# A third staging buffer for gate and up weights in an expert loop, laid over part of the selection tiles

## What is computed

```
scores = sigmoid(xt @ w_router)                    # 16 experts in 4 groups of 4
g_sel  = argmax over groups of the sum of the two best biased scores
gates  = the two best experts of that group, weights normed to sum 1
h = silu(einsum('nd,edf->enf', xt, w_gate)) * einsum('nd,edf->enf', xt, w_up)
h = h * gates.T[:, :, None]                        # D_EXPERT = 256
y = einsum('enf,efd->nd', h, w_down)
```

## Time and profile before

| | us |
|---|---|
| median of 3 runs | 3438.38 |
| lowest, highest | 3436.19, 3446.0 |
| profiled execution | 3443.66 |
| its span | 3441.9 |

### The profile page before, as it was taken

The page is one execution under the profiler, slowest core; times in us unless marked ns, Lnnn a source line. Parts: engine busy times, 40 slices in busy tenths (PEclk is TensorE's granted clock), DMA queues, the critical chain, the costliest instruction groups (busy, mean ns, idle before and its releaser), DMA issues.

```text
span 3441.9 us, 42094 instructions
## 1 busy us (share of the span) xinstructions
PE 3222.5 (94%) x14924; PEld 2551.4 (74%) x14924; DVE 1936.3 (56%) x2968; ACT 1386.9 (40%) x2048; POOL 394.2 (11%) x241
## 2 busy tenths in 40 slices
PE   8899998998999888999988999999999999899998
PEld 6677776676777766888866788877887767678886
DVE  5775776568658765544465644456353553565353
ACT  4553666455536664222223322233222554532221
POOL 3101122331012223000010000010000000010000
PEclk9999999999999999999999999999999999999999
DMA  3101799421018993222312232324233312023232
GB/s 126 48 10 65 236 322 309 132 71 41 19 55 270 323 310 111 83 97 91 98 51 84 71 100 91 101 66 148 90 97 114 108 49 74 25 75 105 85 99 75
DMA packets 174979, 389.59 MB, mean 113 GB/s; under 512 B 11312, under 2 KB 70064, under 8 KB 174192
## 3 DMA queue, kind: packets, MB, share of 16 engines
q1 hardware_dynamic: 173424, 377.45, 33.5%
q0 software_dynamic: 1408, 10.23, 0.8%
HBM read 381.34 MB, written 6.29 MB: 113 GB/s over the span
## 4 chain that ended last, share of the span: by engine, by line
PE 69%; DVE 13%; DMA 9%; ACT 4%; DVEq 2%; issue 2%; POOL 0%; POOLq 0%; ACTq 0%; SPq 0%
PE ps L562 19%; PE ps L564 19%; PE ps L563 19%; DMA gate_up_stage<-in_w_gu 8%; DVE moe_lo L1987 5%; PE ps L751 2%; ACT moe_hi L1170 2%; PE ps L696 1%; PE ps L856 1%; PE ps L729 1%; ACT w_hi L1170 1%; PE ps L687 1%; PE ps L791 1%; PE ps L735 1%; PE ps L809 1%
## 5 line engine op out<-in xcount | busy, mean ns | idle before, releaser
L1601 DVE TENSOR_TENSOR w_lo<-w_stage,w_hi 128x1024 fp32r<-128x1024 f32 (+3 forms) x310 | 398.6, 1287 | 853.9 <-ACT w_hi L1170 852.4
L562 PE MATMUL ps<-xs_hi,w_hi 128*128 128x512 f32 (+2 forms) x1938 | 771.8, 398 | 42.4 <-DVE w_lo L1601 14.7
L1170 ACT ACTIVATE w_hi<-w_stage 128x1024 fp32r<-128x1024 f32 (+3 forms) x350 | 382.3, 1093 | 1013.0 <-PE ps L564 999.3
L564 PE MATMUL ps<-xs_hi,w_lo 128*128 128x512 f32 (+2 forms) x1938 | 765.5, 395 | 0.0
L563 PE MATMUL ps<-xs_lo,w_hi 128*128 128x512 f32 (+2 forms) x1938 | 765.2, 395 | 0.0
L562 PEld LDWEIGHTS ps<-xs_hi,w_hi 128*128 128x128 f32 (+2 forms) x1938 | 365.8, 189 | 141.8 <-issue 22.8
L564 PEld LDWEIGHTS ps<-xs_hi,w_lo 128*128 128x128 f32 (+2 forms) x1938 | 365.9, 189 | 84.2
L563 PEld LDWEIGHTS ps<-xs_lo,w_hi 128*128 128x128 f32 (+2 forms) x1938 | 366.7, 189 | 81.8
L1987 DVE TENSOR_TENSOR moe_lo<-gate_up_stage,moe_hi 128x1024 fp32r<-128x1024 f32 x224 | 270.1, 1247 | 118.7 <-ACT moe_hi L1170 118.1
L1170 ACT ACTIVATE moe_hi<-gate_up_stage 128x1024 fp32r<-128x1024 f32 x224 | 226.4, 1054 | 149.4 <-DMA gate_up_stage<-in_w_gu 139.8
L564 PE MATMUL ps<-h_hi,w_lo 128*128 128x512 f32 x704 | 278.3, 395 | 0.0
(11 more groups left out here) (381 smaller groups left out, 4872.4 us busy)
## 6 DMA issues: line engine op xcount, KB each, us to landing
gate_up_stage<-in_w_gu SPq DMA_DIRECT2D x112, 1024.0 KB, 5.6
w_stage<-in_f_gu SPq DMA_DIRECT2D x174, 512.0 KB, 3.5
down_stage<-in_w_dn SPq DMA_DIRECT2D x112, 512.0 KB, 5.8
w_stage<-in_f_dn SPq DMA_DIRECT2D x64, 704.0 KB, 4.0
w_stage<-in_w_in SPq DMA_DIRECT2D x30, 512.0 KB, 3.6
w_stage<-in_d_qk SPq DMA_DIRECT2D x24, 512.0 KB, 3.5
w_stage<-in_w_out SPq DMA_DIRECT2D x16, 512.0 KB, 3.6
w_stage<-in_d_v SPq DMA_DIRECT2D x12, 512.0 KB, 3.5
```

The lines of the kernel that those rows point to most:

```text
L562: pe.matmul(o, lh, rh, start=start, stop=False)
L564: return pe.matmul(o, ll, rh, start=False, stop=stop)
L1170: copy = lambda o, i: nc.scalar.activation(o, i, ACT.Copy)
L1601: tt(w_lo[:, s, 0:n], stage[:, s, 0:n], w_hi[:, s, 0:n].bitcast(F32), ALU.subtract).then_inc(w_split, 1)
```

## The change

The list of gate and up buffers gets a third, `gate_up_stage2`, of 8 KB a partition. It is placed at the tiles 3 to 6 of `sel_t`, which is also the last 8 KB of `sel`. The transfers, numbered q = 2 st + i, take the buffers 0, 1, 0, 2, 1, 0, 2, 1, ... Each waits for the splitting of the transfer that had its buffer before; the first use of buffer 2 (q = 3) waits for `gt_full`, the last reading of `sel`. On SP `(2, 0)` is issued ahead of the loop, and in the loop the order becomes `(st + 2, 1)`, `down (st + 1, 0)`, `down (st + 1, 1)`, `(st + 3, 0)`. Tiles 0 to 2 of `sel_t` are made in steps 1 to 3 as before; tiles 3 and 4 are made in step 26 and tiles 5 and 6 in step 27, after `moe_lo` unit 4 in step 26 and right after `ht_lo` in step 27. The orders of TensorE, ScalarE and POOL are the same.

```diff
+        gu_stage.append(over(region_s, "gate_up_stage2", [P, 4, 512], at=(NTILES - 4) * T * 4))
...
+        GU_BUFFER = [0, 1] + [(0, 2, 1)[q % 3] for q in range(2 * STEPS - 2)]
+        GU_TURN = [GU_BUFFER[:q].count(b) for q, b in enumerate(GU_BUFFER)]
+        GU_USES = [GU_BUFFER.count(b) for b in range(3)]
...
-        gu_landed = [sem(f"gate_up_landed{i}") for i in range(2)]
+        gu_landed = [sem(f"gate_up_landed{i}") for i in range(3)]
...
                 def gate_up_weights(st, i):
-                    if st > 0:
-                        sp.wait_ge(gu_lo, l * 4 * STEPS + 4 * (st - 1) + 2 * i + 2)
+                    q = 2 * st + i
+                    b = GU_BUFFER[q]
+                    if GU_TURN[q] > 0:
+                        before = max(p for p in range(q) if GU_BUFFER[p] == b)
+                        sp.wait_ge(gu_lo, l * 4 * STEPS + 2 * before + 2)
+                    elif b == 2:
+                        sp.wait_ge(gt_full, l + 1)
...
+                gate_up_weights(2, 0)
                 for st in range(STEPS):
-                    for i in range(2):
-                        if st + 2 < STEPS:
-                            gate_up_weights(st + 2, i)
+                    if st + 2 < STEPS:
+                        gate_up_weights(st + 2, 1)
                     for i in range(2):
                         if st + 1 < STEPS:
                             down_weights(st + 1, i)
+                    if st + 3 < STEPS:
+                        gate_up_weights(st + 3, 0)
...
-                    if 1 <= st <= NTILES:
-                        if st == 1:
-                            v.wait_ge(row_copied, l + 1)
-                        ts(selt[:, st - 1, :], slot_row[:, :], dc[:, C_COL + st - 1:C_COL + st], None, ALU.is_equal).then_inc(selt_ready, 1)
+                    if st == 1:
+                        v.wait_ge(row_copied, l + 1)
+                    for i in {1: (0,), 2: (1,), 3: (2,), STEPS - 2: (3, 4), STEPS - 1: (5, 6)}.get(st, ()):
+                        ts(selt[:, i, :], slot_row[:, :], dc[:, C_COL + i:C_COL + i + 1], None, ALU.is_equal).then_inc(selt_ready, 1)
```

More of the change, by code:

```diff
@@ L159, in build_program, with staged @@
         gu_stage = [over(at_stage, "gate_up_stage0", [P, 4, 512])] + gu_stage
+        gu_stage.append(over(region_s, "gate_up_stage2", [P, 4, 512], at=(NTILES - 4) * T * 4))
         dn_stage = dn_stage + [over(at_stage, "down_stage1", [P, M_SLOT], at=8192)]
-        def staged(u):
+        GU_BUFFER = [0, 1] + [(0, 2, 1)[q % 3] for q in range(2 * STEPS - 2)]
+        GU_TURN = [GU_BUFFER[:q].count(b) for q, b in enumerate(GU_BUFFER)]
+        GU_USES = [GU_BUFFER.count(b) for b in range(3)]
+        def staged(st, u):
             if u < 4:
-                return gu_stage[u // 2][:, :, 256 * (u % 2):256 * (u % 2) + 256]
+                return gu_stage[GU_BUFFER[2 * st + u // 2]][:, :, 256 * (u % 2):256 * (u % 2) + 256]
             return dn_stage[u - 4][:, :].rearrange("p (c n) -> p c n", c=4)
@@ L413, in gate_up_weights @@
                 def gate_up_weights(st, i):
-                    if st > 0:
-                        sp.wait_ge(gu_lo, l * 4 * STEPS + 4 * (st - 1) + 2 * i + 2)
+                    q = 2 * st + i
[5 more added lines that the diff above has]
+                        sp.wait_ge(gt_full, l + 1)
                     src = a["w_gu"][bass.ds(group_of(st // 4) * 16 + (l * 64 + st % 4 * 4), 4), :, 512 * i:512 * i + 512]
-                    sp.dma_start(gu_stage[i][:, :, :], src.rearrange("c p n -> p c n")).then_inc(gu_landed[i], 16)
+                    sp.dma_start(gu_stage[b][:, :, :], src.rearrange("c p n -> p c n")).then_inc(gu_landed[b], 16)
                 def down_weights(st, i):
@@ L422, in down_weights @@
                     src = a["w_dn"][bass.ds(group_of(st // 4) * 8 + (l * 32 + 4 * i), 4), :, 256 * (st % 4):256 * (st % 4) + 256]
-                    sp.dma_start(staged(4 + i), src.rearrange("c p n -> p c n")).then_inc(dn_landed[i], 16)
+                    sp.dma_start(staged(st, 4 + i), src.rearrange("c p n -> p c n")).then_inc(dn_landed[i], 16)
                 for i in range(2):
@@ L1359, in hi @@
                 def hi(st, u):
-                    act.wait_ge(gu_landed[u // 2] if u < 4 else dn_landed[u - 4], 16 * (st0 + st + 1))
+                    if u < 4:
+                        q = 2 * st + u // 2
+                        b = GU_BUFFER[q]
+                        act.wait_ge(gu_landed[b], 16 * (l * GU_USES[b] + GU_TURN[q] + 1))
+                    else:
+                        act.wait_ge(dn_landed[u - 4], 16 * (st0 + st + 1))
                     if st > 0 and u < 4:
@@ L1364, in hi @@
                         act.wait_ge(dn_used, 2 * (st0 + st - 1) + u - 3)
-                    copy(parts(m_hi[u]), staged(u)).then_inc(gu_hi if u < 4 else dn_hi, 1)
+                    copy(parts(m_hi[u]), staged(st, u)).then_inc(gu_hi if u < 4 else dn_hi, 1)
                 def silu(st):
@@ L1986, in lo @@
                         v.wait_ge(dn_hi, 2 * (st0 + st) + 1)
-                    tt(parts(m_lo[u]), staged(u), parts(m_hi[u]).bitcast(F32), ALU.subtract)\
+                    tt(parts(m_lo[u]), staged(st, u), parts(m_hi[u]).bitcast(F32), ALU.subtract)\
                         .then_inc(gu_lo if u < 4 else dn_lo, 1)
```

## The result

The changed kernel took 3405.0 us in the median of 4 runs (3393.7 to 3412.0), beside 3442.2 for the kernel before in the same comparison: ratio 0.9906, 95% interval 0.9881 to 0.9932. It is 37 us faster; 3396 within 3367 to 3433 was forecast. The profiled execution took 3401.1 us, its span is 3399.4, 42.5 less than before.

The account below looks back on a forecast made before the run. The prediction took TensorE to bound the whole kernel and a transfer, copy and subtraction lap the expert loop. Loop gain -50 and end cost +8 gave -42 us: 3396 as the median (3438.4 before), range 3367 to 3433.

Parts of the forecast that it names:

- The bound: Whole kernel bound by TensorE; expert loop by a 9.9 us lap of transfer, copy and two subtractions through single buffers.
- 9.3 us: Expert loop: step length at the old transfer speed if all of the queue's idle 0.07 goes; 10.0 if none.
- less than half: Sign of being right: ScalarE's waits for gate and up transfers fall to less than half of before.
- below 30: Sign of being right: TensorE's wait at line 890, before turning the hidden rows, falls below 30 from 140.5 us.
- Part 1: Third buffer in the expert loop: 9.0 us a step instead of 10.0, gaining 50 us; TensorE's own step is 8.47.
- 8.4 us for a well-fed queue: Expert loop: queue time for a step's transfers at 403 and 358 GB/s, 8.1 us, or 8.4 with the joints.
- Such stretches: Slow transfer stretches in the loop, such as 238 GB/s for 4 us with transfers pending.
- Part 2: Start of the loop: transfer (1, 1) waits some 0.5 us longer, (2, 0) is issued earlier; cost zero.
- Part 3: Moving sel_t tiles 3 to 6 to steps 26 and 27: +4 us a layer at the loop's end, +8 in all.
- (a): Rival: TensorE becomes the loop's bound at 8.5 us a step, 77 us off and 8 on, 3370; chance 0.2.
- (b): Rival: the transfer queue was the loop's bound all along, 9.7 us a step, 3431 (3411 to 3446); chance 0.22.
- (c): Rival: slower; second down transfer's single-buffer lap makes first-half transfers start slowly, 10.2 us a step, 3456; chance 0.12.

Follow-up runs that it names:

- e4: Kernel before plus the third buffer alone, laid over the sums and squares, with sel_t still made in steps 1 to 7: 3404.0 us, ratio 0.9892 to before.
- e1: Changed kernel with sel_t tiles 3 to 6 made in step 26 between h_slot(27) and the subtraction of unit 4: 3400.2 us, ratio 0.9880 to before.
- e11: Changed kernel with every sel_t tile between h_slot and the subtraction of unit 4, in steps 1 to 3 and 26: 3392.6 us, ratio 0.9864 to before.
- e12: e4 with the sel_t tiles of steps 1 to 7 placed between h_slot and the subtraction of unit 4: 3402.1 us, ratio 0.9901 to before.
- e9: Changed kernel with one more, unread 1024 KB transfer in each of steps 1 to 20: one execution of 3491.3 us, 377 GB/s.
- e10: e9 with weights laid out in long runs of 8 KB and 4 KB: one execution of 3441.5 us, 414 GB/s in the first layer.
- e3: Kernel before with only sel_t tiles 3 to 6 moved to steps 26 and 27, no third buffer: 3447.6 us, ratio 1.0015 to before.
- e2: Changed kernel with the gate and up transfer (st + 3, 0) issued ahead of both down transfers: 3419.0 us, ratio 0.9936 to before.

## Why the prediction was right, point by point

**The bound.** Right in this: transfer, copy and subtractions made the chain of the loop, the stall at line 890 was its mark, and the buffer by itself (e4) took most of it away. Wrong was "a further buffer adds no bandwidth", and with it the reading of a busy share of 0.93 as a queue that is nearly full. The rate rose from 312 to 340 GB/s. Of the 0.90 us that a step lost, 0.68 were slow landings and some 0.15 an empty queue, so the transfers of the lap were long because the queue was slow, and the lap and the queue were not two separate bounds. The 9.3 us that I had as the best the old speed allows were passed (9.11). I had said "less than half" for the waits of ScalarE (139.8 to 79.0: not quite) and "below 30" for the wait at the turns (140.5 to 65.7: wrong, counted on both sides), since the step did not come as close to 8.47 as 9.0.

**Part 1, 9.0 us a step.** Measured 9.11, a gain of 45 instead of 50. The number was luck in part. The row it was taken from (turns 1101.47 to 1119.38, which are steps 5 and 6, not 4 and 5) has the length that VectorE gives a step with a slow sel_t: in e4, where these stay in steps 1 to 7, three steps in a row of the second layer take 8.96, 8.95 and 8.95 again. Of the queue it showed only that it can keep up with 9.0 for two good steps. Measured is floor plus slow landings, 8.36 + 0.78, and the 0.78 stood in no row of the prediction. Other kernels with three buffers and the same order of transfers (e1, e4, e11, e12) had 9.17 to 9.34 in their profiled executions. My 8.4 us for a well-fed queue was within 0.1 of the 8.36 which e9 shows. "Such stretches come mostly where a transfer is issued as the queue is about to run empty" agrees with e9, e10 and the first table as far as the place goes, though I later bet on a fixed rate of 340 GB/s and lost. That "the second down transfer still meets a nearly empty queue" came true (14 slow cases of 48, before 2).

**Part 2, the start.** Nothing was lost: turn 0 stands at 370.88 (before 371.76).

**Part 3, the end.** +4 a layer was forecast, +4.4 and +4.2 measured, by the very chain laid out: one sel_t ahead of POOL, one behind it, 4.10 us idle, then half clock. From the end of the subtraction of unit 4 to that of h_turned_lo, 3.6 us were forecast and 3.3 measured (616.38 to 619.67); down(27) began 4.5 us after turn 27, and at full clock the end would have been about 2 us longer than before, against the 2.4 forecast. The half-clock stretch was longer than assumed: 12 matmuls at 0.43 us against 0.23, so 2.4 us of loss instead of 1.5. The gain in steps 4 to 7 was left inside the 9.0; e3 shows that by itself it is worth less than the end costs.

**The sum.** -42 forecast, -42.5 between the profiled spans, -37 between medians. The near hit of the spans is chance: runs of one kernel differ by up to 22 us, which is of the size of some 15 slow landings more or less (1.3 to 1.4 us late in the median).

**The rivals.** (a) needed a queue that is always full; with long runs and a full queue the transfers of a step would take 7.5 us, so TensorE could lead, and no kernel here got there with the given bytes. The 358 GB/s by which the Trainium skill (DMA: Bandwidth & Descriptors, Specifications) would have ended this rival at 8.8 us did not bind: 377 GB/s for 189 us and 414 for 173 us were measured with this one core at work, and the measurement decides. (b) was half right: slow landings are nearly all of the time over the floor before and after, but there are half as many us of them. (c) wanted a slow start in every step. It came in part: the second down transfer was slow in 14 steps of 48. With the other order (e2) the lap of landing, copy and POOL's subtraction, which (c) names, made 90% of the chain of the first layer's loop, and even so the kernel was faster than before.

## What to carry to other kernels

A further buffer can be worth something even where the DMA engines look nearly full: with more transfers queued the queue is never empty, and here it also had fewer slow landings. Look at the distance between landings under full load before blaming the bandwidth: here a step's transfers need 8.36 us (7.48 with longer runs) and took 9.8 and 9.1. And where work is moved to make room, look for the place at which the engine is idle and nobody waits: four sel_t took 1.67 us that nobody waited for in one place, and lengthened the end of each loop by 4.2 to 4.4 us in another. A lap that is not the longest (here that of the second down transfer) comes forward as soon as the order changes (e2) or the others get shorter (e11).

## What the hardware showed that I had not expected

- The rate of the queue depends on how it is fed: 312 GB/s before, 340 in the change, 377 with a third more bytes (2 KB and 1 KB runs). Runs of 8 and 4 KB gave 414 when the queue was full, and 333, no more than the short runs, when it was not.
- A share of 0.97 busy DMA engines was no sign of a queue at its best rate: at 377 GB/s the same measure showed 1.06.
